# A PEER router's weighting step on VectorE: the order in which one multiply walks its 512 elements

## What is computed

```
s1, i1 = top_k(s[:, :, 0], 16);  s2, i2 = top_k(s[:, :, 1], 16)     # 8 heads, 128 keys in each half
idx, top = the 16 best of the 256 sums;   g = softmax(top)
act = gelu(einsum('td,thkd->thk', xb, u[idx]))
out = einsum('thk,thkd->td', g * act, v[idx])
```

## Time and profile before

| | us |
|---|---|
| median of three runs | 2789.27 |
| lowest and highest | 2789.21, 2790.97 |
| span of the profiled execution | 2791.7 |

### The profile page before, as it was taken

One profiled execution on the slowest core, in us unless ns is written; L12 is line 12 of the kernel. 1 busy time (PEld: TensorE's weight loads), 2 busy tenths in 40 slices (PEclk: granted clock), 3 DMA queues, 4 the chain that ended last, 5 costly groups with the idle time before them and its releaser, 6 DMA issues. The chain is left out here.

```text
span 2791.7 us, 50744 instructions
## 1 busy us (share of the span) xinstructions
PE 2530.5 (91%) x17672; PEld 2236.5 (80%) x17672; DVE 1823.1 (65%) x3955; ACT 1552.8 (56%) x3124; POOL 263.3 (9%) x240
## 2 busy tenths in 40 slices
PE   6978999999867999997989998899999976899997
PEld 3658988888756999997765534798899975899997
DVE  6844789866798555557244455349885479755555
ACT  5635655676696555556413542255556579555554
POOL 0000444100000000000001110014440000000000
PEclk8989999999988999999989999999999988999999
DMA  6743444577301455553206986344445510355452
GB/s 235 256 135 139 155 162 152 209 251 260 136 0 47 180 181 180 180 181 126 64 30 247 344 327 243 121 162 155 159 164 175 180 59 0 108 179 181 180 180 106
DMA packets 65102, 455.79 MB, mean 163 GB/s; under 512 B 8656, under 2 KB 8864, under 8 KB 10224
## 3 DMA queue, kind: packets, MB, share of 16 engines
q1 hardware_dynamic: 52128, 379.61, 38.5%
q0 software_dynamic: 11120, 73.29, 6.8%
q10 hardware_dynamic: 1760, 1.68, 0.2%
HBM read 415.27 MB, written 39.27 MB: 163 GB/s over the span
## 5 line engine op out<-in xcount | busy, mean ns | idle before, releaser
L824 ACT ACTIVATE w_parts<-ring 128x512 fp32r<-128x512 f32 x1376 | 851.4, 630 | 856.0 <-PE ps L423 767.0
L1199 DVE TENSOR_TENSOR w_parts<-ring,w_parts 128x512 fp32r<-128x512 f32 x1232 | 853.8, 704 | 606.1 <-ACT w_parts L824 597.3
L423 PE MATMUL ps<-h_hi,w_parts 128*128 128x264 f32 x5376 | 1022.7, 289 | 83.3 <-DVE w_parts L1199 58.0
L423 PEld LDWEIGHTS ps<-h_hi,w_parts 128*128 128x128 f32 x5376 | 854.9, 191 | 123.7 <-issue 68.7
L423 PE MATMUL ps<-h_lo,w_parts 128*128 128x264 f32 x2688 | 770.7, 287 | 0.0
L423 PE MATMUL ps<-g_parts,w_parts 128*128 128x264 f32 x6144 | 749.6, 284 | 7.5 <-DVE g_parts L1495 7.5
L423 PEld LDWEIGHTS ps<-g_parts,w_parts 128*128 128x128 f32 x6144 | 749.3, 189 | 7.8 <-issue 7.8
L423 PEld LDWEIGHTS ps<-h_lo,w_parts 128*128 128x128 f32 x2688 | 515.4, 192 | 2.0
L423 PE MATMUL ps<-SCR 128*128 128x128 f32 x1056 | 185.5, 331 | 92.4 <-DVE SCR L1466 85.2
L1126 POOL TENSOR_TENSOR w_parts<-ring,w_parts 128x512 fp32r<-128x512 f32 x144 | 210.9, 1466 | 479.6 <-ACT w_parts L824 479.2
L423 PEld LDWEIGHTS ps<-SCR 128*128 128x128 f32 x1056 | 158.9, 231 | 118.8 <-issue 87.9
(11 more groups left out here) (176 smaller groups left out, 1473.3 us busy)
## 6 DMA issues: line engine op xcount, KB each, us to landing
ring<-in_stream SPq DMA_DIRECT2D x362, 1024.0 KB, 4.8
BIG<-in_C POOLq DMA_DIRECT2D x32, 1024.0 KB, 8.5
out_C_s<-BIG POOLq DMA_DIRECT2D x32, 1024.0 KB, 5.9
out_C_p<-BIG POOLq DMA_DIRECT2D x16, 256.0 KB, 2.3
x<-in_x ACTq DMA_DIRECT2D x1, 1056.0 KB, 15.0
out_y<-BIG POOLq DMA_DIRECT2D x1, 1056.0 KB, 4.2
consts<-in_consts ACTq DMA_DIRECT2D x1, 256.0 KB, 10.4
BIG<-in_gates POOLq DMA_DIRECT2D x1, 192.0 KB, 2.7
```

Of the source, the lines that this page charges most:

```text
L423: return nc.tensor.matmul(out, lhsT, rhs, start=start, stop=stop, skip_group_check=shared)
L824: return nc.scalar.activation(to, of, f, **kw_)
L1199: tt(w_lo[:, j % HALVES, :], half_of(n, half), w_hi[:, j % HALVES, :].bitcast(F32), ALU.subtract).then_inc(lo_ready[half], 1)
```

## The change

Only the order in which `weigh` walks its operands is changed. Before, the four tokens are the outer dimension and the 128 rows the inner one: the reads of PSUM are contiguous, and the reads and writes of `G` step 264 elements. After, the 128 rows are the outer dimension and the four tokens the inner one: `G` is read and written in runs of four neighbours, and the reads of PSUM step 128 elements (512 bytes) within a run. The elements, the products, the number of instructions and every wait stay the same.

```
     def weigh(g, s):

-        Gt = G[:, :, bass.ds(g * 4, 4)].rearrange("p r t -> p t r")
-        tt(Gt, ps[:, s, :].rearrange("p (t r) -> p t r", t=4), Gt, ALU.mult).then_inc(routed[l], 1)
+        Gt = G[:, :, bass.ds(g * 4, 4)]
+        tt(Gt, ps[:, s, :].rearrange("p (t r) -> p r t", t=4), Gt, ALU.mult).then_inc(routed[l], 1)
```

## The result

The changed kernel takes 2759.55 us (median of four runs, 2758.6 to 2760.5), beside 2789.47 us for the kernel before: a ratio of 0.9888 with a 95% interval of 0.9874 to 0.9902, 30 us or 1.1% less. The forecast was 2758 us.

A forecast was written before the change was run, and what follows sets the result against it. VectorE was taken to bound the routing stage, with ScalarE next at 1.833 us a group. Gains of 16.2 and 16.6 us, together 32.8, lowered to 31 for lower-clock stretches, gave 2758 us; range 2753 to 2785 us.

The forecast's parts named there:

- The bound of the kernel before: Routing stage: VectorE sets the end at 2.01 us a group, with ScalarE 0.18 us a group behind it.
- The price of the new weigh: Weigh in routing: falls from 1102 ns to 691 to 830 ns, with PSUM steps costing 0 to 36 ns.
- a quarter of the surcharge: Weigh's walk of G: if big steps cost the 411 ns, at most 103 ns is left, giving 794 ns.
- The cap: Routing stage: ScalarE becomes the bound at 1.833 us a group, capping a gain of up to 54 us.
- The sum: Both routing stages: gains of 16.2 and 16.6 us, together 32.8 us, lowered to 31 us for lower-clock stretches.
- The clock: TensorE in routing: lower clock about a quarter of the time, mostly made good through four buffers; 31 us gain expected.
- Dear PSUM steps: Rival, weigh's PSUM read: pays the surcharge G shows now, weigh 1205 ns, 2803 us; 11%.
- the exchange: Rival, weigh: surcharge moves whole to PSUM or the walk is not the cost; 1.06 to 1.14 us, 2789 us; 6%.
- the half gain: Rival, weigh: comes to 0.9 to 1.05 us, VectorE stays the bound, 2771 to 2781 us; 5%.
- TensorE at the lower clock: Rival, routing: lower clock through most of the stage, TensorE sets 2.05 us a group, 2783 us at worst; 6%.

The follow-up runs named there:

- runs of two: Changed kernel with weigh walking two neighbouring tokens innermost, then the rows, then the other two tokens: 2757.38 us, ratio 0.9876.

## Why the prediction was right

- **The bound of the kernel before.** Shown. VectorE alone set the end: 0.4 us a group less for ScalarE changed nothing there (ratio 1.0003).
- **The price of the new weigh.** 691 to 830 ns were forecast, 692 ns measured. For PSUM the near row, line 1653, was the right one to trust, though it is another operation with a shorter step, so that this was a guess until the 692 ns. Reads 512 bytes apart, none next to the one before it, cost as much as contiguous ones. The rule of the Trainium skill ("Advanced Engine Details and Errata", section "Memory Cachelines", PSUM part), that every two consecutive elements should be contiguous, does not show in VectorE's time here. Its SBUF part says that a line has to be hit at least twice to hide the access time; 692 ns with runs of two against 1102 ns with none agrees with that. I did not use that part, and used a quarter of the surcharge as a bound, which the runs of two refute; the forecast did not need it.
- **The cap.** Shown twice over: a weigh that is 0.07 us longer costs nothing, and less work for ScalarE gives 31 us. The full 54 us that 132 x 0.411 promise were not to be had while ScalarE needs 1.83 us a group.
- **The sum.** 122.9 us in each layer from ScalarE's first build to the last weigh; the forecast was 866.5 - 743.47 = 123.0 us and 2379.2 - 2256.16 = 123.0 us. The 32.8 us were measured as 33.0 us in the two stages and as 29.9 us between the medians; the forecast of 31 us lies between. The 1.8 us that it took off for stretches at the lower clock were not lost in the stages, so that it comes nearer to the medians than 32.8 us does is luck.
- **The clock.** Here the right number stands on a step that was put to the test only at the start of each layer. I expected about a quarter of the time at the lower clock, made good from the four buffers. In fact most of that time went: after the start of each layer (0.83 from 2240 to 2260 us) the windows show a granted clock of 1.00. What was left was made good: VectorE caught up at some 1.62 us a group, and the stage of layer 1 took 122.9 us like that of layer 0. Whether longer or later stretches would have been made good, no run shows. As a cause of the whole gain the clock is excluded: 0.18 us a group, 24 of the 33 us, are the difference between ScalarE's own pace, 1.83 us at either clock, and VectorE's steady 2.01 us, read where the granted clock was 1.00. The other 9 us are what the kernel before lost over its steady pace (2.07 and 2.08 us a group in the mean), for the most part in its stretches at the lower clock. Whether the slack or the higher clock gave these back, the runs do not separate.
- **The rivals.** Dear PSUM steps, the exchange and the half gain fell with the 692 ns. TensorE at the lower clock occurred only at the start of each layer. Its price was worked out wrongly: 132 x 0.02 us and two weighs shorter by 0.4 us are 3.4 us, so its worst case is 2786 us and not 2783, just outside the range.

## What to carry to other kernels

For an elementwise instruction over two layouts, ask in which operand neighbours are lost, and put the short run where the price is shown: in this multiply a run of two was enough in SBUF, and 512-byte steps in PSUM cost nothing. Before adding up such gains, read the free pace of the engine next in line and take the difference to that; here it cut 54 us to 31. When two engines have changed places as the bound, see whether a small share of work can move between them: here one token in sixteen gave another 16 us. And read who released an engine against the waits in the program: a row can name an instruction that this wait does not need.

## What the runs showed of the hardware that I had not expected

- VectorE's 128x512 multiply with 1056-byte steps took 1082 ns with the steps in the read alone, 1089 ns in the write alone and 1102 ns in both, against 692 ns without: the two prices are not added.
- With the steps in the write alone the next instruction on VectorE started 0.15 to 0.19 us before the end, with steps in the read 0.07 to 0.12 us before it: equal durations, groups of 1.93 and 2.01 us.
- TensorE's granted clock in the routing windows of layer 0 was 0.87 to 0.90 with routes every 2.01 us, 0.95 to 0.96 with 1.93 us (in layer 1 of that kernel 1.00 from 2260 to 2300 us and 0.83 from 2300 to 2340 us), and 1.00 with 1.83 us or less, at 25.16 busy us in 40 after the change against 26.50 before (which counts slower matmuls). What the clock follows was not tried.
